# Weaving the second block's mixing: projections, scan, attention groups and output product in one order, and the scan's products on GpSimd

## The reference

```python
proj = h @ w_in                       # 1024 -> 2472 columns
a_q, a_k, a_v, b_cq, b_ckv, b_kr, c_z, c_xbc, c_dt = split(proj)
# differential attention: 4 heads, two softmaxes of width-32 scores, V of 64
p = softmax(mask(s1)) - lam * softmax(mask(s2))
y_a = rmsnorm(p @ v, subln_g) * (1 - lambda_init)
# MLA: 4 heads, latent q and kv, 64 + 32 roped columns, V of 64
y_b = softmax(mask(q @ k)) @ v
# mamba2: causal convolution of width 4, silu, scan over 8 heads, gate, norm
y_c = rmsnorm((scan(xs, dt, a, B, C) + d_skip * xs) * silu(c_z))
y = concat([y_a, y_b, y_c]) @ w_out
x = x + g_m * rmsnorm(y)
```

## Time and profile before

| | |
|---|---|
| runs of the kernel before | 3535.72, 3539.12, 3542.89 us; median 3539.12 |
| profiled execution, its time | 3541.45 us |
| its span (first to last instruction) | 3539.7 us |
| mean granted TensorE clock | 0.913 of full speed |
| busy: PE / DVE / ACT / POOL | 3192.5 / 1755.1 / 705.4 / 832.0 us |
| mixing of the second block, layer 0 | 1859.16 to 2247.96 us of the span |
| mixing of the second block, layer 1 | 2708.68 to 3090.90 us of the span |

### The profile page before, as it was taken

One profiled execution on the slowest core, in us unless ns is written; L12 is line 12 of the kernel. 1 busy time (PEld: TensorE's weight loads), 2 busy tenths in 40 slices (PEclk: granted clock), 3 DMA queues, 4 the chain that ended last, 5 costly groups with the idle time before them and its releaser, 6 DMA issues.

```text
span 3539.7 us, 33580 instructions
## 1 busy us (share of the span) xinstructions
PE 3192.5 (90%) x12312; PEld 2192.8 (62%) x12312; DVE 1755.1 (50%) x3758; ACT 705.4 (20%) x1539; POOL 832.0 (24%) x704
## 2 busy tenths in 40 slices
PE   6877989999987788999979998899997998899996
PEld 3334548888733454888864452488884444378886
DVE  1375337775327543777542265495833347152343
ACT  2233320000113332000012241220202133121110
POOL 0120113444312011344430000144340000124442
PEclk8987799999998788999999978899998978899998
DMA  4111313443211001344221100144420210112221
GB/s 194 57 39 72 143 60 113 173 179 110 90 48 48 24 1 60 130 156 183 106 76 67 71 1 0 72 172 161 179 103 28 76 48 1 48 48 95 77 91 48
DMA packets 38546, 304.89 MB, mean 86 GB/s; under 512 B 4192, under 2 KB 4320, under 8 KB 23920
## 3 DMA queue, kind: packets, MB, share of 16 engines
q1 hardware_dynamic: 38352, 302.68, 23.3%
q0 software_dynamic: 32, 0.07, 0.0%
HBM read 300.63 MB, written 2.10 MB: 86 GB/s over the span
## 4 chain that ended last, share of the span: by engine, by line
PE 78%; DVE 11%; issue 4%; ACT 3%; DMA 2%; POOL 1%; DVEq 0%; SPq 0%; POOLq 0%; ACTq 0%
PE bank L950 43%; PE bank L928 16%; PE bank L1039 4%; PE bank L1294 1%; DVE SPT L2265 1%; PE bank L1147 1%; PE bank L1089 1%; PE bank L1278 1%; PE bank L1076 1%; PE bank L1026 1%; DMA ring<-in_slabs 1%; DVE sel L1931 1%; PE bank L1285 1%; PE bank L1013 1%; DVE m L1930 1%
## 5 line engine op out<-in xcount | busy, mean ns | idle before, releaser
L855 POOL TENSOR_TENSOR SPT<-ring 128x512 f32<-128x512 f32 (+2 forms) x140 | 170.3, 1216 | 1863.3 <-DMA ring<-in_slabs 1244.6
L928 PE MATMUL bank<-hT,ring 128*128 128x512 f32 (+1 forms) x960 | 422.2, 599 | 14.6 <-ACT hT L1604 6.5
L950 PE MATMUL bank<-U,ring 128*128 128x256 f32 x1728 | 406.5, 380 | 0.0
L950 PEld LDWEIGHTS bank<-U,ring 128*128 128x128 f32 x1728 | 326.3, 190 | 43.3
L928 PEld LDWEIGHTS bank<-hT,ring 128*128 128x128 f32 (+1 forms) x960 | 181.3, 190 | 252.1 <-issue 246.1
L1750 DVE SCALAR_TENSOR_TENSOR nw<-sel,c,nw 128x256 f32<-128x256 f32 x504 | 321.8, 638 | 23.2 <-DMA sel<-in_mod_pieces 5.5
L950 PE MATMUL bank<-hT,ring 128*128 128x256 f32 x1216 | 299.8, 397 | 22.4 <-ACT hT L1604 8.6
L950 PE MATMUL bank<-U,SPT 128*128 128x256 f32 x1296 | 311.2, 379 | 0.1
L950 PE MATMUL bank<-hT,SPT 128*128 128x256 f32 x1216 | 287.3, 379 | 0.0
L950 PEld LDWEIGHTS bank<-hT,ring 128*128 128x128 f32 x1216 | 230.3, 195 | 70.9 <-issue 17.2
L950 PEld LDWEIGHTS bank<-U,SPT 128*128 128x128 f32 x1296 | 246.2, 190 | 33.9 <-POOL SPT L860 0.5
(11 more groups left out here) (293 smaller groups left out, 4164.6 us busy)
## 6 DMA issues: line engine op xcount, KB each, us to landing
ring<-in_slabs SPq DMA_DIRECT2D x88, 2048.0 KB, 8.0
sel<-in_mod_pieces SPq DMA_DIRECT2D x144, 512.0 KB, 3.8
ring<-in_slabs SPq DMA_DIRECT2D x8, 1536.0 KB, 7.1
ring<-in_slabs SPq DMA_DIRECT2D x8, 1280.0 KB, 6.0
ring<-in_slabs SPq DMA_DIRECT2D x4, 1664.0 KB, 7.0
ring<-in_slabs SPq DMA_DIRECT2D x2, 1808.0 KB, 7.3
cst<-in_consts SPq DMA_DIRECT2D x1, 2120.0 KB, 24.3
ring<-in_slabs SPq DMA_DIRECT2D x2, 1056.0 KB, 5.3
```

The source lines that it names most:

```text
L855: pool.tensor_tensor(e1, a21, a22, ALU.add).then_inc(*pool_order.up())
L928: mm = pe.matmul(dst, lhs(k), rhs(k), start=(k == 0), stop=(k == n - 1))
L950: mm = pe.matmul(into[j][:, c:c + HALF], lhs[:, k, :], rhs[:, k, :], start=(begin and k == 0), stop=(end and k == kp - 1))
```

## The change

It rewrites `order2` with `woven`, and what hangs on it:

- The `xbc` projections and convolutions come first (B and C move from the `mix` slab to a slab with v, `bv`, for which a ring slot gets 64 more columns). Then the other projections except A_q/A_k are woven with the whole scan.
- Attention goes by groups of up to four heads (`GROUPS2`: six MLA groups, twelve differential ones). MLA groups are woven with the A_q/A_k projections and `sz`/`sn`; differential groups with the first half of `wo`.
- The scan's multiplication by `G` moves from VectorE to GpSimd. `G` and the decays lie packed (1280 columns), in buffers for three heads.
- Rows are no longer normalised before the transposes. `pv` now uses the transposed weights as stationary operand and gives 64 output columns a head; `on` scales the result (for "d" by the root of its own norm, so `asq`/`an` go), and `ot` transposes it back.
- `wo` is split over its input rows: `("wo", 0, n)` takes the scan's four tiles, `("wo", 1, n)` the attention's four, and VectorE adds the two. `ys` has no matmuls any more: GpSimd adds the squares, and `post` has one ones-matmul.
- Each kind of step has its own small group of banks.

```diff
+    for n in range(6, 10):
+        o += [st for c in tile2(n) for st in c] + [("conv", n - 6)]
+    for n in (4, 5):
+        o += [st for c in tile2(n) for st in c] + [("conv", n)]
+    o += [("projv", 0), ("projv", 1), ("projv", 2), ("projv", 3), ("dt",), ("silu", 0)]
+    dense = [c for n in range(4) for c in tile2(n)]
+    dense[8] += [("cqss",)]
+    dense += [[("kvss",), ("kr",)]]
+    dense += [c for n in range(10, 14) for c in tile2(n)]
+    dense += [[("silu", 1)]] + [[("mq", h)] for h in range(4)] + [[("mk", h)] for h in range(4)]
+    dense += [[("mqr", h)] for h in range(4)] + [[("mv", i)] for i in range(QT)]
+    scans = [[("dtt",)]] + [[("xd", i)] for i in range(QT)] + [[("G", g, st)] for g in range(2) for st in range(QT)]
+    scans += [[("da", 0)]]
+    for h in range(10):
+        if h < 7:
+            scans.append([("da", h + 1)])
         if h < 8:
+            scans += [[("scan", h, st)] for st in range(QT)]
+        if 0 <= h - 1 < 8:
+            scans.append([("y", h - 1)])
+        if 0 <= h - 2 < 8:
+            scans.append([("yo", h - 2)])
+    o += woven((0.0, 1.0, dense), (0.1, 1.0, scans))
+    slots = group_slots2(range(len(GROUPS2)))
+    keys = [c for n in range(14, 18) for c in tile2(n)]
+    o += woven((0.0, 1.0, keys), (0.0, 0.4, [[("sz",)], [("sn", 0)], [("sn", 1)]]),
+               (0.1, 1.0, [c for slot in slots[:NM2] for c in slot]))
+    o += woven((0.0, 1.0, [[("wo", 0, n)] for n in range(KT)]), (0.0, 1.0, [c for slot in slots[NM2:] for c in slot]))
...
+GROUPS2 = [("m", 0, 4, 0), ("m", 0, 4, 1), ("m", 0, 2, 2), ("m", 2, 2, 2), ("m", 0, 2, 3), ("m", 2, 2, 3)]
+GROUPS2 += [("d", h, 2, i) for i in (0, 1) for h in range(2)] + [("d", h, 1, i) for i in (2, 3) for h in range(4)]
+def group_slots2(groups):
+    out = []
+    for j in range(len(groups) + 3):
+        slot = []
+        if j < len(groups):
+            slot.append([("sc", groups[j])])
+        if 0 <= j - 1 < len(groups):
+            if GROUPS2[groups[j - 1]][0] == "d":
+                slot.append([("cb", groups[j - 1])])
+            slot.append([("tp", groups[j - 1])])
+        if 0 <= j - 3 < len(groups):
+            slot.append([("on", groups[j - 3])])
+        if 0 <= j - 2 < len(groups):
+            slot.append([("pv", groups[j - 2])])
+        if 0 <= j - 3 < len(groups) and groups[j - 3] in TURNS2:
+            slot.append([("ot", groups[j - 3])])
+        out.append(slot)
+    return out
...
+    if kind == "da":
+        return [(st, ROWS[:1])]
+    if kind in ("xd", "G"):
+        return [(st, ROWS[1:])]
...
 # VectorE
-                        link(dve.tensor_tensor_scan(x, tmp[:, h % 2, P * s:SEQ],
-                                                    cst[:, C_DELTA:C_DELTA + SEQ - P * s], 0.0, ALU.mult, ALU.add))
-                        dve.tensor_tensor(x, x, U[:, GT[h // 4][s], P * s:SEQ], ALU.mult).then_inc(*s2["m"].up())
+                        dve.tensor_tensor_scan(x, tmp[:, h % 2, P * s:SEQ], cst[:, C_DELTA:C_DELTA + SEQ - P * s], 0.0,
+                                               ALU.mult, ALU.add).then_inc(*s2["dc"].up())
...
 # GpSimd
             for l in range(DEPTH):
+                for h in range(8):
+                    for s in range(QT):
+                        g = 1280 * (h // 4)
+                        x = mixing[h % 3][:, tri[s]:tri[s + 1]]
+                        pool.wait_ge(*s2["dc"].after(l, QT * h + s + 1))
+                        pool.tensor_tensor(x, x, flat_x[:, g + tri[s]:g + tri[s + 1]], ALU.mult).then_inc(*s2["m"].up())
+                add_squares(l, 0)
                 for n in range(len(FFN2)):
                     slab_sums(2, l, n)
+                add_squares(l, 1)
```

More of the change, by code:

```diff
@@ L27 @@
 SLAB = 4096
+SLOT = SLAB + 64
 RING = 2
@@ new lines, with turn_of @@
+NM2 = len(GROUPS2)
+GROUPS2 += [("d", h, 2, i) for i in (0, 1) for h in range(2)] + [("d", h, 1, i) for i in (2, 3) for h in range(4)]
+TURNS2 = [g for g, (c, h, nh, i) in enumerate(GROUPS2) if c == "m" or h % 2]
+MO = (CQ, CQ + 1)
+Y0 = [XRAW + t for t in range(6)] + [MQ, MQ + 1]
+SUMS2 = [(("cqss",), 0), (("cqss",), 1), (("kvss",), 1), (("sn", 0), 0), (("sn", 0), 1), (("sn", 1), 0), (("sn", 1), 1)]
+NS2 = len(SUMS2)
+SUMS2 += [(("post", 0), 1)] * KT + [(("post", 1), 1)] * KT
+def turn_of(g):
+    return next(k for k, t in enumerate(TURNS2) if t >= g)
@@ L465, in order2, with tile2 @@
+def tile2(n):
+    return [[("proj", 3)]] if n == 3 else [[("pj", n, 0)], [("pj", n, 1)], [("pj", n, 2)], [("proj", n)]]
 def order2(l):
     o = [("prep",), ("ns", 0), ("nh", 0)]
[L467 to L470, removed]
@@ L1171, in _ @@
                     kind = st[0]
-                    jobs = jobs2(st)
                     if kind != "unit":
-                        for job, _ in jobs:
+                        for job, _ in jobs2(st):
                             pe.wait_ge(*bk2.before(l, job))
-                    if kind == "ys":
-                        jobs = [(("post", 0), SIDE)]
-                    if jobs:
-                        dst = bank[bk2.bank(l, jobs[0][0])]
-                        done = (full[bk2.bank(l, jobs[0][0])], 1)
+                    home = bk2.bank(l, st) if bk2.has(l, st) else None
+                    dst = bank[home] if home is not None else None
+                    done = (full[home], 1) if home is not None else None
                     if kind == "mm":
@@ new lines, in _ @@
+                        if n == 0 and s == 0:
+                            pe.wait_ge(*s2["hn"].after(l, 7))
+                        elif n == 0:
+                            for g in TURNS2:
+                                pe.wait_ge(*bk2.taken(l, ("ot", g)))
+                        pe.wait_ge(*sl2.ready(l, ("wo", s)))
+                        w4 = ring[:, sl2.slot(l, ("wo", s)), :].rearrange("p (k n) -> p k n", k=4)
+                        right = [U[:, XC + t, :] for t in range(4)] if s == 0 else [hT[:, 0, :], hT[:, 1, :], U[:, MO[0], :],
+                                                                                  U[:, MO[1], :]]
@@ L1658, in _ @@
-                        if c == "d":
-                            ins = act.activation(sel[:, u % 3, 0:n], sel[:, u % 3, 0:n], ACT.Exp,
-                                                 bias=stat[:, 3:4], scale=scale, accum_out=stat[:, 5:6])
+                        stat = statD[:, g % 4, :]
+                        act.wait_ge(*s2["sc"].after(l, g + 1))
+                        for hh in range(nh):
+                            for half in range(2 if c == "d" else 1):
+                                s = (rowS, row2)[half][g % 2][:, n * hh:n * hh + n]
+                                k = 4 * half + hh
+                                ins = act.activation(s, s, ACT.Exp, bias=stat[:, 8 + k:9 + k], scale=scale,
+                                                     accum_out=stat[:, 16 + k:17 + k])
```

562 lines of the change are left out of this document (321 added, 241 removed).

## The result

The changed kernel takes 3598.02 us (median of 4 runs, 3594.39 to 3600.3) beside 3537.42 us for the kernel before on the same chip: ratio 1.0164, 95% interval 1.0147 to 1.0181. It is 60 us slower. The forecast was 3499 us, 40 us faster, with a range up to 3555; the time lies outside it, and on the side that had a chance of 0.14.

A forecast was written before the change was run, and what follows sets the result against it. TensorE, busy 90% of the span, was taken as the bound. Stages 56+117+57+98+31.5 plus 6 behind gave 365.5 against 385.5 us a layer, 40 less in all: 3541.45-40, less 2.3, is 3499 us; range 3435 to 3555.

The forecast's parts named there:

- stage D: Half of wo woven with twelve differential groups in fifteen slots: 98 us a layer (75 to 135).
- I add 3 for a mild loss: In stage D, 3 us added to 95 at full clock because TensorE's clock won't be full.
- the loop of 5.2 us a slot: In stage D, masks, combine, transposes, copy, root, scaling and mean, not overlapped by other slots: 5.2 us, 0.7 more with ot.
- C: A_q/A_k projections woven with six MLA groups, gate and sn: 57 us a layer (50 to 66).
- The exposed tiles: In stage D, six of eight wo tiles not hidden in TensorE's waits: 22 us added.
- The check from outside: First block's woven tail takes 1.6 times its TensorE work; C and stage D's 100 us would give 160, against 155 forecast.
- Stage B: Other projections woven with the whole scan: 108 us of TensorE work plus stalls, 117 us a layer (107 to 132).
- The tail wait: End of Stage B, TensorE left with cheap work while the last heads are scanned: 5 us (0 to 20).
- The upper bound taken for GpSimd: In Stage B, VectorE's scans and GpSimd's products run one after the other: 7.5 us a head.
- Stage E: Eight half tiles of wo, then add, square, last sum and one ones-matmul: 31.5 us a layer.
- Behind: After the mixing, GpSimd's slab sums beside VectorE's post loop stretch it by 6 us a layer (0 to 10).
- Rival 3: Slower: stage D runs at half clock, 135 us, 402 a layer, 3573 us in all; chance 0.13.

The follow-up runs named there:

- e4: Changed kernel plus extra matmuls with unused results where TensorE waits in stage D, except where a tile of wo stands; 3555.5 us, ratio 1.0037.
- e9: Changed kernel with earlier combine, wo in pieces, mean a slot later, root ahead of exponentials, scaling behind masks, two banks for the values; 3459.0 us.
- e1: Changed kernel with combine of group j-1 and scaling of j-3 moved ahead of group j's masks and exponentials; 3533.5 us, ratio 0.9968.
- e11: Changed kernel with the sums of differential weights with the values taking turns in two banks; 3563.1 us, ratio 1.0061.
- e2: Changed kernel with the eight tiles of wo's first half behind all groups instead of between them; 3611.5 us, ratio 1.0193.
- e5: Changed kernel with wo's first-half tiles cut in four matmuls, spread over stage D's slots, copied by ScalarE a slot later; 3524.9 us, ratio 0.9960.
- e3: Changed kernel with the scan's products moved back from GpSimd to VectorE, order unchanged; 3605.4 us, ratio 1.0173.
- e8: Changed kernel with GpSimd's first two slab sums ahead of the sums of squares again; 3583.7 us, ratio 1.0133.

## Why the prediction was wrong

The direction was wrong through one term, stage D. The other stages came within 7% of their terms.

- **Stage D (98, measured 132).** Two steps of it failed. The first is "I add 3 for a mild loss" of clock: it was at least 20.5 us (e4). The clock itself was foreseen, "near 0.75" by the earlier trace rows, and it was 0.73; its price was too small by a factor of seven. 0.73 is a mean of the levels 1.2 and 2.4 GHz, about half of the stretch at each, and the matmuls that take 61 us at full clock (e9) take 87. This is 17.5 of the 34 us. The other 16.5 us are missing at full clock, 95 against 111.5 (e4), and the step that failed there is the loop of 5.2 us a slot. It began with the masks and ended with the scaling and the mean. It left out TensorE's own links between the scaling and the next masks: the values and `ot`, 1.06 us at full clock (2188.12 to 2189.18 in e4), and the next scores, 1.26 until the first mask. The slot takes 7.12, where I had 5.9 with `ot`; 1.2 us more in each of fifteen slots is about the 16.5. That these steps form one loop is shown by e1, which opens it by order alone and gives 36 us; the bank of the values adds a wait of 1.3 us a slot to it, 17 us (e11). TensorE's work in D was too small as well, 50 against 61.4 (e9). A part of that is a slip: the values are 112 matmuls, not 80, because those of the last two MLA groups fall into D. I had taken them out of C ("without the parts that slip into D") and put them nowhere.
- **The exposed tiles (22).** The windows of e2 differ by 22 too, but that is luck in part: they differ in clock as well (0.73 and 0.53), and no run has the tiles' exposure at full clock. Nor is the cost a fate of the work: cut in four, put in the holes and copied later, the tiles give 31 to 33 us back in the same order (e5).
- **The check from outside.** I took the factor 1.6 of the first block over C and D together and got 160 against my 155. Measured is 190. The factor wasn't far off: with the work as the traces have it, 61.4 in D and 52.3 in C, it is 1.7, if the 89 us of the first block hold. What was too small is the 100 us of work that I multiplied, which the sum and its check had in common.
- **Stage B (117, measured 124).** The tail wait was forecast at 5 and is 5.97; the waits of `xd` and `G` were put at 5 and are some 4. The miss is TensorE's busy time, 114 instead of 108, at a clock of 0.97. The upper bound taken for GpSimd did no harm, since B does not hang on it (e3). GpSimd's products are busy 36.9 us a layer, a little over the 28 to 35 foreseen.
- **Stage E (31.5, measured 33.4)**: it begins at the low clock that D leaves. After a D at full clock it is 31.8 (e9).
- **Behind (+6, measured +6)**, by the mechanism named: e8 takes it away.
- **Rival 3** (D 135 at half clock, 3573) came nearest, within 3 us in D, but with half its mechanism. Its clock of 0.54 did not come: it priced the clock at 39 us a layer, where e4 has 20.5 at 0.73, and kept the loop that was too short. The two errors cancel, which is luck. The 25 us between its 3573 and the result are mostly the 7 a layer in B, the 2 in E and the 5 ahead of the block. I gave it 0.13 because "the tiles are long, dense stretches". They are, and they raise the clock of D from 0.53 (e2) to 0.73; but in a slot of 8.5 without one TensorE stands for 4.3 us.

## What to carry to other kernels

In a software pipeline where every engine walks the same list, write down the loop link by link from one bank's filling to its next, the matmuls in it too; then ask of each engine which step of its own list stands needlessly ahead of what another waits for. Here, each alone, two steps moved were worth 36 us of 132, a second bank 17, and cutting dense tiles so that they fit in the waits, with a later copy, 31. Price idle time on TensorE twice, once as waiting and once as the clock it takes from the work around it. The share of idle time alone doesn't give that price: the kernel before has a clock of 0.54 with TensorE busy 90% of its differential stage, the changed one 0.73 with it busy 66% of D. And weave dense work in pieces of the size of the holes, with its evictions later in the list than its last matmul (in this case the two were only tried together).

## What the runs showed of the hardware that I had not expected

Adding 33 us of useless matmuls to a stage made it 20.5 us shorter (e4), because the granted clock went from 0.73 to 0.97.

VectorE's scans and GpSimd's products both read two SBUF tensors, and where they met, which one lost followed who had started first (e3): a 384-wide scan 0.16 us ahead of a product kept its 0.93 us while the product took 1.83 instead of some 1.28, and a 256-wide scan that started 0.69 us behind took 1.69 instead of 0.69. The mean of a group hides this: the 512-wide scans rose from 1.22 to only 1.30 us because most of them met no product.
